# Keys and queries in 4 KB rows of scratch, corners gathered on the chip, and the next head's loads behind the first loop of a hybrid decoder step

## The reference, cut to what matters

```python
a_mat = jnp.where(strict, jnp.einsum('bhnid,bhnjd->bhnij', kb, k) * decay, 0.0)
sol = lax.linalg.triangular_solve(jnp.eye(C) + a_mat, rhs, left_side=True, lower=True, unit_diagonal=True)
attn = jnp.einsum('bhnid,bhnjd->bhnij', q, k) * decay
# scan over chunks: v_new = u - w S;  o = q_dec S + attn v_new;  S = S * gl + k_dec v_new
```

## Time and profile before

| | us |
|---|---|
| median of three runs | 1975.99 (1963.57 to 1976.21) |
| the profiled execution | 1957.82, of which span 1956.1 |
| mean granted TensorE clock, share of full | 0.928 |
| TensorE busy | 1742.1 (89%) |
| VectorE, ScalarE, POOL busy | 818.9, 640.1, 355.2 |
| projection, first loop of the mixers, head 0 starts | until 841, 841 to 952, 965 |
| DMA | 309.58 MB, mean 158 GB/s, under 512 B 69404 of 250314 packets |

### The profile page before, as it was taken

The page is one execution under the profiler, slowest core; times in us unless marked ns, Lnnn a source line. Parts: engine busy times, 40 slices in busy tenths (PEclk is TensorE's granted clock), DMA queues, the critical chain, the costliest instruction groups (busy, mean ns, idle before and its releaser), DMA issues. The chain is left out here.

```text
span 1956.1 us, 27679 instructions
## 1 busy us (share of the span) xinstructions
PE 1742.1 (89%) x9686; PEld 1434.6 (73%) x9686; DVE 818.9 (42%) x1888; ACT 640.1 (33%) x1550; POOL 355.2 (18%) x372
## 2 busy tenths in 40 slices
PE   5999999999999999946698898898899569889896
PEld 5998888888888888834587788788788447666674
DVE  3535323511541252134664444443443455445462
ACT  4534222411321241110233444344345223333342
POOL 0000000000000000034033421422432342333231
PEclk9999999999999999977698998898898659999999
DMA  5425686877458767689657456546322466665660
GB/s 169 133 57 152 155 249 168 174 193 208 142 152 247 178 149 208 196 212 234 169 130 177 118 117 162 137 108 157 109 62 74 118 181 196 210 172 172 161 198 27
DMA packets 250314, 309.58 MB, mean 158 GB/s; under 512 B 69404, under 2 KB 198940, under 8 KB 240716
## 3 DMA queue, kind: packets, MB, share of 16 engines
q1 hardware_dynamic: 250196, 308.02, 59.2%
HBM read 228.50 MB, written 146.44 MB: 192 GB/s over the span
## 5 line engine op out<-in xcount | busy, mean ns | idle before, releaser
L339 PE MATMUL pj<-hT_hi,w_hi 128*128 128x512 f32 x896 | 361.8, 404 | 1.8 <-DVE raw L592 1.8
L340 PE MATMUL pj<-hT_lo,w_hi 128*128 128x512 f32 x896 | 354.6, 396 | 0.0
L341 PE MATMUL pj<-hT_hi,w_lo 128*128 128x512 f32 x896 | 354.3, 395 | 0.0
L341 PEld LDWEIGHTS pj<-hT_hi,w_lo 128*128 128x128 f32 x896 | 168.4, 188 | 40.8
L339 PEld LDWEIGHTS pj<-hT_hi,w_hi 128*128 128x128 f32 x896 | 168.6, 188 | 39.6 <-issue 2.1
L340 PEld LDWEIGHTS pj<-hT_lo,w_hi 128*128 128x128 f32 x896 | 168.7, 188 | 36.8
L1154 POOL TENSOR_TENSOR gm<-upto,g_hi 128x512 fp32r<-128x512 f32 x16 | 16.6, 1040 | 875.8 <-POOLq L2557 839.1
L1400 PE MATMUL o_ps<-pt,vt 128*65 128x256 f32 (+3 forms) x560 | 149.9, 394 | 3.1 <-DVE ot L1649 2.1
L1491 ACT ACTIVATE pt<-pt_ps 128x512 f32<-128x512 f32 x144 | 84.7, 589 | 165.3 <-PE pt_ps L1378 165.0
L2283 PE MATMUL y_bank<-wo_hi,mh 128*128 128x512 f32 (+1 forms) x272 | 113.2, 416 | 6.8 <-POOL ml L2268 4.6
L2285 PE MATMUL y_bank<-wo_hi,ml 128*128 128x512 f32 (+1 forms) x272 | 110.7, 407 | 0.0
(11 more groups left out here) (458 smaller groups left out, 3554.6 us busy)
## 6 DMA issues: line engine op xcount, KB each, us to landing
out_dram<-in_cache_k_win_dram SPq DMA_DIRECT2D x56, 584.0 KB, 8.7
out_dram<-in_cache_v_win_dram SPq DMA_DIRECT2D x56, 584.0 KB, 8.3
w_raw<-in_w_in_dram SPq DMA_DIRECT2D x31, 512.0 KB, 12.4
qk_ch<-sil SPq DMA_DIRECT2D x32, 256.0 KB, 4.7
z_ch<-xr SPq DMA_DIRECT2D x32, 256.0 KB, 4.7
wqk<-hi SPq DMA_DIRECT2D x32, 256.0 KB, 5.2
wqk<-lo SPq DMA_DIRECT2D x32, 256.0 KB, 5.4
sc_class<-qk_ch SPq DMA_DIRECT2D x32, 256.0 KB, 5.2
```

What stands on the lines that cost most here:

```text
L339: pe.matmul(out, w_hi[s][:, k, :], hT_hi[:, k, cols], start=(k == 0), stop=False)
L340: pe.matmul(out, w_hi[s][:, k, :], hT_lo[:, k, cols], start=False, stop=False)
L341: mm = pe.matmul(out, w_lo[s][:, k, :], hT_hi[:, k, cols], start=False, stop=(k == KT - 1))
```

## The change

1. Scratch for keys and queries becomes one tensor ordered by chunk, [16, 128, 4, 2, 128]; a chunk is read by one load with 4 KB per partition. The stores write it in pieces of 512 B. The gates za of the delta part get the same treatment ([16, 128, 4, 128], 2 KB per partition on reading); zb keeps its rows.
2. The corners are not read back from nt. POOL multiplies nt by a mask that keeps each row's own block of 16 (128 x 512 elements), VectorE adds up the eight blocks into [128, 4, 16], and SP stores that in rows of 256 B (32 KB a chunk). After the loop one load brings all corners into 128 partitions with 4 KB each. The mask `own` is built in chunk 1 and not 8; the padding of nt's rows in HBM is gone.
3. The loads of the next head (queries and keys of head 1, tokens, gates, keys and queries of delta chunks 0 and 1) move from chunks 9, 11 and 13 behind the loop and the corner load. The near and class values move from chunks 5 and 7 to chunks 10 and 13, and head 0's queries and keys from behind the second ring load to behind the fifth.

```diff
-                        sp.dma_start(D.qk_ch[y, rows, cs], sil[:, c, :]).then_inc(sil_stored[c], 16)
+                        sp.dma_start(D.kq[NCH * c:NCH * c + NCH, :, j, 1 - y].rearrange("n p t -> p n t"), sil[:, c, :].rearrange("p (n t) -> p n t", t=P)).then_inc(sil_stored[c], 16)
...
+                            sp.dma_start(D.za[NCH * c:NCH * c + NCH, :, j].rearrange("n p t -> p n t"), zr[:, c % 2, :].rearrange("p (n t) -> p n t", t=P)).then_inc(z_stored[c % 2], 16)
...
-QK_DMAS, V_DMAS, KQ_DMAS, CHUNK_DMAS = 6, 4, 2, 6
+QK_DMAS, V_DMAS, KQ_DMAS, CHUNK_DMAS = 6, 4, 1, 5
...
-    for half_, y in ((0, 1), (1, 0)):
-        sp.dma_start(kq[:, :, half_, :], D.qk_ch[y, :, bass.ds(P * c, P)].rearrange("(h p) t -> p h t", p=P)).then_inc(into, 16)
+    sp.dma_start(kq.rearrange("p h x t -> p (h x t)"), D.kq[bass.ds(c, 1)].rearrange("a p h x t -> (a p) (h x t)")).then_inc(into, 16)
...
-                sp.dma_start(corner[NB * c:NB * c + NB], blocks[:, :, :, 0:BASE]).then_inc(S["corner_in"], 16)
+            def store_corner(c):
+                sp.wait_ge(S["corner_made"], c + 1)
+                sp.dma_start(D.corner.rearrange("(c p x) -> c p x", c=NT, p=P)[c], flat(diag[c % 2][:])).then_inc(corner_out[c % 2], 16)
...
-                if c == 5:
+                if c == 10:
                     load_near_v_from(sp, D, E, 0)
-                if c == 7:
+                if c == 13:
                     load_class_v_from(sp, D, E, 0)
-                if c == 9:
-                    load_qk_from(sp, D, E, 1, 1)
-                if c in (11, 13):
-                    load_tokens_from(sp, D, E, c // 2 - 5, c // 2 - 5)
-                    load_kq_from(sp, D, E, c // 2 - 5, kq[c // 2 - 5], chunk_in[c // 2 - 5])
...
+            store_corner(NT - 1)
+            for e in range(2):
+                sp.wait_ge(corner_out[e], 16 * NT // 2)
+            sp.dma_start(corner.rearrange("p j h i -> p (j h i)"), D.corner.rearrange("(p x) -> p x", p=P)).then_inc(S["corner_in"], 16)
+            load_qk_from(sp, D, E, 1, 1)
+            for e in range(2):
+                load_tokens_from(sp, D, E, e, e)
+                load_kq_from(sp, D, E, e, kq[e][:], chunk_in[e])
...
+            def mask_corners(c):
+                pool.wait_ge(S["nt_made"], c + 1)
+                if c >= 2:
+                    pool.wait_ge(S["corner_made"], c - 1)
+                own = E.own[:].unsqueeze(1).unsqueeze(3).to_broadcast([P, H, NB, BASE])
+                pool.tensor_tensor(masked_nt[c % 2], nt[c % 2][:].rearrange("p h (b i) -> p h b i", b=NB), own, ALU.mult).then_inc(S["own_masked"], 1)
...
+                if c >= 2:
+                    mask_corners(c - 2)
...
                 if c >= 2:
+                    dve.wait_ge(S["own_masked"], c - 1)
                     dve.wait_ge(nt_out[u], 16 * (c // 2))
...
+            def gather_corners(c):
+                dve.wait_ge(S["own_masked"], c + 1)
+                if c >= 2:
+                    dve.wait_ge(corner_out[c % 2], 16 * (c // 2))
+                dve.tensor_reduce(diag[c % 2][:], masked_nt[c % 2].rearrange("p h b i -> p h i b"), AX.X, ALU.add).then_inc(S["corner_made"], 1)
...
                 prepare(c)
+                if c:
+                    gather_corners(c - 1)
...
+            gather_corners(NT - 1)
```

More of the change, by code:

```diff
@@ L927, in mixers @@
         half = sb("halves", [P, H])
+        diag = [sb(f"diag{e}", [P, H, BASE]) for e in range(2)]
         half_gb = sb("gb", [NS, H, DEC_BATCH])
@@ L944, in mixers @@
         key_at, row_at, tok_at = tri[:, 3, 0:2].rearrange("p h t -> p (h t)").bitcast(I32), tri[:, 3, 2, 0:1].bitcast(I32), tri[:, 3, 2, 1:2]
+        corner_out = [sem(f"corner_out{e}") for e in range(2)]
+        masked_nt = [t[:].rearrange("p l h t -> p (l h t)")[:, small:small + H * P].rearrange("p (h b i) -> p h b i", h=H, b=NB) for t in cross]
         head_stored, sum_stored = sem("head_stored"), sem("sum_stored")
@@ L1044, in head @@
                     if ahead:
-                        load_kq_from(sp, D, env, c + 2, kq[u], chunk_in[u])
+                        load_kq_from(sp, D, env, c + 2, kq[u][:], chunk_in[u])
                         load_attn(c + 2, u)
@@ L1136, in block_masks @@
                 select(odd, ALU.not_equal, -1.0, 0, [[-2, P // 2]], 1)
-                then(pool.memset(E.own[:], 1.0))
-                select(E.own[:], ALU.is_ge, 0.0, 0, [[-BASE, NB]], 1)
-                select(E.own[:], ALU.is_ge, 0.0, BASE - 1, [[BASE, NB]], -1)
                 then(pool.memset(E.below[:], 1.0))
@@ L1169, in _ @@
                         pool.memset(solved[:, j, :, j:j + 1], 1.0).then_inc(S["eye_set"], 1)
+            for c in (NT - 2, NT - 1):
+                mask_corners(c)
             pool.memset(state[:], 0.0).then_inc(S["state_made"], 1)
```

33 lines of the change are left out of this document (17 added, 16 removed).

## The result

| | before | after |
|---|---|---|
| median, us | 1974.26 (1963.57 to 1976.21, 4 runs) | 1949.51 (1943.64 to 1953.99, 4 runs) |
| ratio | | 0.9883, 95% from 0.9845 to 0.9922 |
| profiled execution, us | 1957.82 | 1950.58 (span 1948.9, clock 0.926) |
| TensorE, VectorE, POOL busy, us | 1742.1, 818.9, 355.2 | 1751.9, 836.4, 371.9 |

The kernel became faster by 1.2% (0.8 to 1.6), 24.7 us between the medians. 1956 was forecast, 1940 to 1974 as the range. Of all executions behind this document one, the profiled one of c_u2, ran at a mean granted clock of 0.712 and took 2267 us; it is in no median and no ratio here, and c_u2 has no row in the table of the experiments.

What follows compares the result with a forecast made beforehand. Transfers were taken to bound the mixers' first loop, TensorE the projection. Terms -3 + 0 - 19 + 1.5 + 1 gave -19.5 us, 1938.3 in the profiled execution, carried to a median of 1956; range 1940 to 1974.

Steps and rivals of the forecast that it cites:

- first stall: Wait before chunk 2: keys and queries in 4 KB, not 512 B, rows save 3 us (0 to 3.8).
- chunks 2 to 7: VectorE-busy stretch: near values leave -2.9, reduces +2.2 after a 1.4 us fill of waits, mask collisions +0.7; together 0.
- chunks 7 to 15: 54.5 us become 35.5: 25.4 of VectorE work, 4.0 of store waits, 6.1 for value loads; -19.0 (-29 to -6).
- behind the loop: After chunk 15 two reduces in a row, the last needing POOL's mask, lie on the path: +1.5 us.
- moved loads: Loads behind the loop delay the inverse's store and loads back; first microsecond of lateness hidden: +1 us (0 to +2).
- projection: 48 stores in 512 B rows take 0.4 us more each, 19 us of queue time hidden by TensorE's products: 0.
- the waits for the store of two chunks before: Chunks 7 to 15: mean wait 1.39 us, of which the reduce fills 0.72, leaving 0.67 x 6 = 4.0 us.
- The first rival: The stores' landing sets each loop chunk and reduces fill nothing: chunks 7 to 15 gain 6.3 us, 1969; chance 0.20.
- no waits at all: Best end for chunks 7 to 15: only VectorE's 25.4 us of work remain, -29 us.
- The rival: Moved loads run over: at 220 GB/s throughout, the inverse is stored at T + 41, +5.0 instead of +1, 1961; chance 0.12.
- the T + 52 that I had called wrong: Sign against the forecast: TensorE's second set of cross products, then expected at T + 49.7, later than T + 52.
- the slower rival: Scattered 512 B stores at half rate, 127 GB/s, hold up the projection: 44 us, 2000; chance 0.06.

Runs made afterwards that it cites:

- c_u2: u2_corners once more, unchanged, as the measure on the same chip: 1930.83 us against 1966.11 of the kernel before, ratio 0.9824 (0.9797 to 0.9850).
- the repetition: The changed kernel run once more, unchanged, beside the kernel before on one chip: 1939.59 us against 1964.03, ratio 0.9871 (0.9851 to 0.9891).
- u2_corners: The changed kernel without part 2: no mask, reduce or corner store, each chunk's corners read back from nt; 1934.96 us, ratio 0.9843 to the kernel before.
- o3_loads: The kernel before with part 3 alone (the moved loads), layouts and corners left as they were: 1942.11 us, ratio 0.9876.
- u1_rows: The changed kernel without part 1: old stores in 2 KB rows, two loads of 512 B rows per chunk; 1946.64 us, ratio 0.9909 to the kernel before.
- u3_loads: The changed kernel without part 3, the moved loads put back into the loop: 1958.22 us against 1968.07 of the kernel before, ratio 0.9959.
- w2_spread: u2_corners with values behind the loop, delta chunk 1's tokens and keys later, head 0's loads singly behind stores of chunks 1 to 6: 1947.22 us, 0.9908.

## Why the prediction was right, and where it was off

**The place and the mechanism were right.** The loop lost its foreign loads, VectorE's waits went, and the saving came from there. That chunk 15 starts at 927.13, where 927 was forecast, is luck: the mixers began 3.5 us later than before, and counted from their first load chunk 15 gained 26.4 us where the terms forecast 22. The forecast added -19.5 us to the profiled time and carried it to the median; the mixers gave -24.0 up to the inverse (-22.3 in the repetition), the medians -24.7. With 1.2% (0.8 to 1.6) the comparison does not tell whether the 1% line was passed, on which the chances stood nearly even; the repetition, 1.3% (1.1 to 1.5), lies beyond it. The terms, as the prediction put them:

| term | forecast | measured |
|---|---|---|
| first stall | -3 | -4.2 (-3.0 in the repetition) |
| chunks 2 to 7 | 0 (-3 to +4) | +3.7 (23.6 to 27.2) |
| chunks 7 to 15 | -19.0 (-29 to -6) | -25.8 (54.5 to 28.7) |
| behind the loop | +1.5 | +2.3 (chunk 15 to the inverse: 34.7 to 37.0) |
| moved loads | +1 | 0 (inverse to second cross set: 16.8 to 16.9) |
| projection | 0 | +3.5 and +1.3 in the two profiles, within the scatter; no run shows a loss |

**The reduce was mis-sized.** 0.72 us came from a reduce of 484 elements; 0.68 would have been right for a reduce that reads in a row, and this one takes 1.02. Five of them are +5.1 and not +3.6, and the fill of 1.4 us that I took off did not come: u2_corners shows 5.5 us between chunks 2 and 7. Behind the loop 1.93 and not 1.44.

**Chunks 7 to 15: waits and reduces do not add.** I had 25.4 us of work and 10.1 of waits beside it. The work was 8 x 3.39 = 27.1 us (3.18 a chunk forecast; the slower reduce alone adds 0.3), and beside it stands one wait of 1.5 us. The step that failed is "the waits for the store of two chunks before ... 0.67 x 6" and the 6.1 us for the value loads: a longer chunk covers the store's landing and the values' traffic whole. u2_corners has no reduces and the same 29 us. The first rival, that the landing sets each chunk (1969), is out, and the bound "no waits at all" (-29) was nearer than my value.

**The first stall** is set by the 3.15 MB of head 0 ahead of chunk 0's store: with these behind the store, chunk 2 starts at 15.5. What the rows add is small beside it and lies in the scatter. With head 0's loads ahead, the four profiles with 512 B rows have chunk 2 at 27.7 to 30.5 (mean 29.6), the seven with 4 KB rows at 26.1 to 29.3 (mean 27.3). The forecast -3 is near the difference of the means, 2.3, and the pairs disagree: o3_loads with short rows has 27.7, u2_corners with long ones 29.3.

**The moved loads** did about what I had worked out for them. I had the queue empty at T + 32 to T + 37.5 (T is the end of chunk 15, now 928.9 us); the last of them landed at T + 37.9, behind the first store of the inverse at T + 35.2 (34.4 forecast). The load back came 0.6 us later for it, and that was hidden, as the first microsecond was in the forecast. The rival was near, though. In u1_rows, where keys and queries come in two loads of 512 B rows, zb was issued 26.5 us behind the end of chunk 15 instead of 16.5, and the load back of the inverse followed its second store by 6.0 us instead of 3.4. The second set of cross products came at T + 52.1, just beyond the T + 52 that I had called wrong: 1.9 us of it are the two reduces, not the loads.

**A rule beside the trace.** The Trainium skill (SBUF — State Buffer, section Who interferes with whom) says that a reduce never contends with POOL on this chip; the trace agrees: all 16 took 0.995 to 1.042 us, and a POOL operation ran beside every one of them. VectorE waited once for the mask, 0.3 us. For the slower rival I had named what the Trainium skill (DMA: Bandwidth & Descriptors, section Latency and other measured facts) tells of rows large powers of two apart. At the 512 KB of this kernel its own row has 207 GB/s against a full 214; the half rate stands there for 4 and 8 MB, so it did not speak for the rival. No run here slows by it: TensorE had 693.4 busy us of the projection's 695, above the 688 named.

**The terms and the whole.** The two large errors, 6.8 us too little gained in chunks 7 to 15 and 3.7 too much in chunks 2 to 7, have opposite signs; the sum was 4.5 us short, and 1956 lay 6.5 us off. What I did not see at all is that beside part 3 the second part costs more than it brings (114.4 without it, 119.2 and 120.9 with it), so that up to the inverse the whole change is worth less than its third part alone (119.2 against 114.7). Without part 3 it brings 1.8 us there.

## What to carry to other kernels

Where one queue holds both the stores that free buffers and loads for later, price each foreign load by its own transfer time in front of the store: six loads of 0.52 MB were 16.1 us, and moving them was one line. What it is worth to replace a transfer depends on what binds the stretch: while transfers bound the loop, gathering the corners on the chip gained 1.8 us at the inverse, and once the loads were moved the gather cost 4.8 to 6.5. So measure each part again in the final order, beside the whole. Where an engine and the queue take turns as the bound, do not add their costs chunk by chunk but take the larger one, and where the DMA engines are near 0.99, expect a new order to move a stall and not to remove it.

## What the runs showed of the hardware that I had not expected

- A reduce of 128 x 512 to 128 x 64 takes 1.02 us reading in steps of 16 elements and 0.68 reading in a row; POOL's product 1.15 us writing in steps of 8, 1.06 in a row.
- The run time follows the mean granted clock: of u3_loads' twelve executions the fastest had 0.930 and 1950.27 us, the slowest 0.920 and 1974.27. After the same pause of 5.5 us in head 1 TensorE was at its 1.2 GHz level for 10.2 to 17.1 us in twelve profiles and for 30.7 in one, the last 25.3 of these without a gap in its work. That is as much as the part of a change that one profile can show, so a term is read from the stretch in which it lies.
- The stores of za took 12 us to land in the median, in 2 KB rows (11.9 in u1_rows) as in pieces of 512 B (12.1 in the changed kernel), while those of keys and queries took 4.4 to 5.3 in either shape: the shape of the rows matters little here. One profile with pieces, w2_spread, had 7.5 for za with the same projection. What sets the difference between the two kinds was not tested.
- Issuing and landing came far apart behind the loop of the changed kernel, with the DMA engines at 0.90: the last load of attn landed 15.5 us after its issue, where the store of the inverse in the kernel before landed after 2.8.
